# Which engine makes the low parts of the weight slabs in the first block's projections, and how densely the index work is packed

## The reference, cut to what matters

```
u = rmsnorm(h, attn_norm[l])
aq, ak, av, iq, ik, iw, bq, bk, bv, cq, ck, cv, gates = split_columns(u @ w_in)
qa, ka, iqr = rope(aq), rope(ak), rope(iq)
ikr = rope(rmsnorm(ik))
# for each block of 128 queries:
rel   = relu(iqr . ikr * 64**-0.5)              # 8 index heads
score = sum over heads of iw * rel, causal
idx   = top_k(score, 128)                       # the 128 keys that branch A may see
```

## Time and profile before

| what | us |
|---|---|
| median of three runs (lowest, highest) | 3960.11 (3956.6, 3968.04) |
| the profiled execution's own time | 3949.7 |
| its span | 3947.9 |
| busy in the span: PE, DVE, ACT, POOL | 3495.5, 1724.7, 1390.2, 926.9 |
| GpSimd's low parts of these slabs (L448), 32 of them | 148.9 |
| VectorE's low parts of these slabs (L448), 4 of them | 2.29 each |

### The profile page before, as it was taken

One profiled execution on the slowest core, in us unless ns is written; L12 is line 12 of the kernel. 1 busy time (PEld: TensorE's weight loads), 2 busy tenths in 40 slices (PEclk: granted clock), 3 DMA queues, 4 the chain that ended last, 5 costly groups with the idle time before them and its releaser, 6 DMA issues. The chain is left out here.

```text
span 3947.9 us, 53824 instructions
## 1 busy us (share of the span) xinstructions
PE 3495.5 (89%) x22008; PEld 2731.5 (69%) x22008; DVE 1724.7 (44%) x2477; ACT 1390.2 (35%) x2022; POOL 926.9 (23%) x477
## 2 busy tenths in 40 slices
PE   6978998999798789899979979679997988869997
PEld 4755786888576568688857549558884836748885
DVE  6686334322369643441323544444413544443433
ACT  5536332322354443232324342244313343224422
POOL 3327001444342620044433220011102321011100
PEclk9989999999999899999989979889998978979999
DMA  3200221222121022222222000212222100012221
GB/s 126 86 22 24 82 99 71 102 86 96 74 86 43 1 81 101 76 87 96 96 92 86 22 1 4 75 54 96 96 75 81 65 0 2 24 64 85 96 96 53
DMA packets 38648, 266.57 MB, mean 68 GB/s; under 512 B 4784, under 2 KB 5040, under 8 KB 7472
## 3 DMA queue, kind: packets, MB, share of 16 engines
q1 hardware_dynamic: 38448, 263.74, 18.8%
HBM read 261.63 MB, written 2.10 MB: 67 GB/s over the span
## 5 line engine op out<-in xcount | busy, mean ns | idle before, releaser
L1150 POOL TENSOR_TENSOR w_lo_f<-raw_f,w_hi_f 128x2048 fp32r<-128x2048 f32 x64 | 296.0, 4624 | 910.7 <-ACT w_hi_f L360 910.7
L372 PE MATMUL ps<-u_hi,w_hi_d 128*128 128x512 f32 x832 | 327.7, 394 | 93.1 <-DVE w_lo_d L366 54.0
L373 PE MATMUL ps<-u_lo,w_hi_d 128*128 128x512 f32 x832 | 326.6, 392 | 0.0
L374 PE MATMUL ps<-u_hi,w_lo_d 128*128 128x512 f32 x832 | 326.3, 392 | 0.0
L366 DVE TENSOR_TENSOR w_lo_d<-raw_d,w_hi_d 128x2048 fp32r<-128x2048 f32 x74 | 169.5, 2292 | 283.6 <-ACT w_hi_d L360 283.6
L372 PEld LDWEIGHTS ps<-u_hi,w_hi_d 128*128 128x128 f32 x832 | 158.1, 190 | 129.5 <-DVE w_lo_d L366 55.6
L372 PE MATMUL ps<-u_hi,w_hi_f 128*128 128x512 f32 x512 | 202.9, 396 | 33.2 <-DVE u_lo L350 33.1
L360 ACT ACTIVATE w_hi_d<-raw_d 128x2048 fp32r<-128x2048 f32 x74 | 140.9, 1907 | 247.0 <-PE ps L374 241.1
L360 ACT ACTIVATE w_hi_f<-raw_f 128x2048 fp32r<-128x2048 f32 x64 | 122.5, 1914 | 264.3 <-PE ps L374 249.6
L851 POOL TENSOR_SCALAR sc<-sc,small 128x768 f32<-128x768 f32 (+4 forms) x144 | 174.2, 1225 | 155.3 <-DVE small L916 155.3
L374 PE MATMUL ps<-u_hi,w_lo_f 128*128 128x512 f32 x512 | 203.8, 398 | 0.0
(11 more groups left out here) (375 smaller groups left out, 8175.8 us busy)
## 6 DMA issues: line engine op xcount, KB each, us to landing
raw_d<-in_w SPq DMA_DIRECT2D x74, 1024.0 KB, 4.8
raw_f<-in_w SPq DMA_DIRECT2D x64, 1024.0 KB, 4.8
raw_c<-in_w SPq DMA_DIRECT2D x40, 1088.0 KB, 5.0
raw_a<-in_w SPq DMA_DIRECT2D x36, 1024.0 KB, 4.8
raw_p<-in_w SPq DMA_DIRECT2D x24, 1024.0 KB, 4.9
cst<-in_cst SPq DMA_DIRECT2D x1, 2112.0 KB, 8.0
h<-in_x SPq DMA_DIRECT2D x8, 256.0 KB, 4.4
mla_w<-in_w SPq DMA_DIRECT2D x2, 1024.0 KB, 6.8
```

The source lines that it names most:

```text
L372: nc.tensor.matmul(out, w_hi, x_hi, start=start, stop=False)
L373: nc.tensor.matmul(out, w_hi, x_lo, start=False, stop=False)
L374: return nc.tensor.matmul(out, w_lo, x_hi, start=False, stop=stop)
L1150: nc.gpsimd.tensor_tensor(WF[2][:, k % 2, :], WF[0][:, k % 2, :], WF[1][:, k % 2, :].bitcast(F32), ALU.subtract).then_inc(S["w_lo"], 1)
```

## The change

`INDEX_AT` becomes 8 + i // 2, so two pairs of index heads follow each of the tiles n = 8 to 13, on all three engines. VectorE makes up to three picks after a tile. All low parts are made by VectorE: those of slabs 0 and 1 at the start, that of slab 2 after the rope of tile 1, and those of later slabs each in the place that `split_a_hi` has in ScalarE's order: after the ropes, index work and picks of slab i comes the low part of slab i + 3. GpSimd makes only the low parts of the activations.

```diff
-            INDEX_AT = [8 + i for i in range(len(INDEX))]
+            INDEX_AT = [8 + i // 2 for i in range(len(INDEX))]
+            def index_after(n):
+                return [INDEX[i] for i, at in enumerate(INDEX_AT) if at == n]
...
             def slab_ready(pe, i):
-                if i < 2:
-                    pe.wait_ge(S["w_lo"], i + 1)
-                else:
-                    pe.wait_ge(S["slab_lo"], i - 1)
+                pe.wait_ge(S["w_lo"], i + 1)
...
-            def split_a_lo(eng, i, done):
-                eng.wait_ge(S["w_hi"], i + 1)
-                eng.tensor_tensor(WA_lo[:, i % 4, :], WA_raw[:, i % 4, :], WA_hi[:, i % 3, :].bitcast(F32), ALU.subtract)\
-                   .then_inc(done, 1)
+            def split_a_lo(dve, i):
+                if i < len(SLABS):
+                    dve.wait_ge(S["w_hi"], i + 1)
+                    nc.vector.tensor_tensor(WA_lo[:, i % 4, :], WA_raw[:, i % 4, :], WA_hi[:, i % 3, :].bitcast(F32),
+                                            ALU.subtract).then_inc(S["w_lo"], 1)
...
                 @block.gpsimd
                 def _(pool):
                     split_u_lo(pool, four)
-                    for i in range(2, len(SLABS)):
-                        split_a_lo(nc.gpsimd, i, S["slab_lo"])
...
                     rope_bank(0, 1)
+                    split_a_lo(dve, 2)
...
-                    for n, t in enumerate(TILES):
-                        if n < 2:
-                            continue
-                        rope_bank(n, t)
-                        if n - 1 in INDEX_AT:
-                            index(*INDEX[INDEX_AT.index(n - 1)])
-                        for _ in range(2):
-
-                            if row is not None and n - 1 >= INDEX_AT[row * IDX_HEADS // 2 - 1]:
-                                row = next(picks, None)
+                    for i, k in enumerate(SLABS):
+                        if i in VPAIR:
+                            split_a_lo(dve, i + 3)
+                            split_a_lo(dve, i + 4)
+                        elif i - 1 not in VPAIR:
+                            for t in (2 * k, 2 * k + 1):
+                                if not 1 < t < N_QK:
+                                    continue
+                                n = TILES.index(t)
+                                rope_bank(n, t)
+                                for at in index_after(n - 1):
+                                    index(*at)
+                                for _ in range(3):
+
+                                    if row is not None and n - 1 >= INDEX_AT[row * IDX_HEADS // 2 - 1]:
+                                        row = next(picks, None)
+                            split_a_lo(dve, i + 3)
```

More of the change, by code:

```diff
@@ L420, in build @@
                         n = TILES.index(t)
-                        if n in INDEX_AT:
-                            b, hp = INDEX[INDEX_AT.index(n)]
+                        for b, hp in index_after(n):
                             for e in range(2):
@@ L509, in _ @@
                                 n = TILES.index(t)
-                                if n in INDEX_AT:
-                                    index(*INDEX[INDEX_AT.index(n)])
+                                for b, hp in index_after(n):
+                                    index(b, hp)
                 @block.scalar
@@ L587, in _ @@
                     own = Signal(dve_own)
-                    split_a_lo(nc.vector, 0, S["w_lo"])
-                    split_a_lo(nc.vector, 1, S["w_lo"])
+                    split_a_lo(dve, 0)
+                    split_a_lo(dve, 1)
                     dve.wait_ge(loaded, 16)
```

## The result

The changed kernel takes 3972.72 us (median of 8 runs, 3965.41 to 3983.85); the kernel before, over 8 runs, 3961.74. The ratio is 1.0033, 95% interval 1.0017 to 1.0048: **slower by 0.33%**, a little and clearly. The forecast was 3961, no change; the measured time lies outside its near range of 3951 to 3969 us and at the very end of the wide one of 3945 to 3973. The kernel was run again twice for the experiments: ratios 1.0018 (1.0004 to 1.0031) and 1.0036 (1.0023 to 1.0049).

What follows compares the result with a forecast made beforehand. TensorE, busy 89% of the span, was taken as the bound, VectorE close behind. Layers +1.7 and +0.2, attention -2, clock +1.5 sum to +1.4, giving 3961 us; range 3951 to 3969, 8 in 10 from 3945 to 3973.

Steps and rivals of the forecast that it cites:

- The relief of VectorE: VectorE's steps with two SBUF inputs stop being held up: some 2 us or more per low part.
- V0 without a stall: Before V0 in layer 1, TensorE's 2.4 us stall goes, with 0.8 us to spare; V0 ends at 111.2.
- Rival C: Slab 5's low part comes late, V0 starts up to 2.4 us late as now: 3965; chance 0.07.
- The banks: Five banks per tile of n = 8 to 13 make five TensorE bubbles, some 9 us per layer.
- VectorE's sum: VectorE's work from tile 10's swap to slab 17's low part: 117.2 us, leaving a 19 us stall before V1.
- The third pick: Three picks per tile from n = 10: last of 48 made at n = 25, no tail left.
- The clock in the bubbles: Clock falls from the five bubbles cost 0 to 8 us per layer; +1.5 taken for both layers together.
- the 0.9 that the prediction names as a sign of being wrong: The prediction calls itself wrong if the clock in 125 to 170 us falls below 0.9.
- rival B: Index tiles' bubbles make TensorE's clock fall; ten falls cost 8 us per layer, about 3975; chance 0.10.
- VectorE's waits: Between V0 and V1, VectorE idles about 2 us waiting for the swaps of tiles 12 and 14.
- The attention's start: Without 15 us of idle TensorE before it, the attention gains 1 us per layer by the clock: -2.
- The median: The runs' median lies 10.4 above the profiled execution of 3949.7; that difference is carried over to the forecast.

Runs made afterwards that it cites:

- e3: The changed kernel with two picks per tile instead of three; 3947.42 us, ratio 0.9972 to the kernel before.
- e7: The changed kernel with slab i + 3's low part ahead of the picks of slab i's last tile; 3966.75 us, ratio 1.0011 to the kernel before.
- e5: The kernel before with VectorE making all low parts, one pair of heads and two picks per tile; 3936.46 us, ratio 0.9933.
- e10: The changed kernel with two picks per tile, and two pairs of heads only after tiles 8 and 9; 3926.61 us, ratio 0.9934 to the kernel before.
- e6: The kernel before with three picks per tile and nothing else of the change; 3954.49 us, ratio 0.9982.
- e8: The changed kernel with heads read before the swap and added before the rope, two picks per tile; 3936.77 us, ratio 0.9927 to the kernel before.

## Why the prediction was wrong, point by point

*The relief of VectorE.* Right. The rope's middle step (now L601) is held up nowhere, by the groups of VectorE from 111.5 to 262 us, where its mean was 1.61:

```profile
L601 DVE TENSOR_TENSOR four<-four,sin 128x512 f32<-128x512 f32 x17 | 11.6, 681 | 0.0
```

*V0 without a stall.* Right: TensorE goes on without a break, and V0's last values come at 111.6 us (111.2 forecast). Rival C did not occur.

*The banks.* Right in kind and place: five bubbles of 1.1 to 1.9 us, forecast 1.5 to 2. Together they are 7.2 us and not 9.

*VectorE's sum.* Right. From 135.6 to 261.9 us it does what I counted as 117.2 us in 117.7 (126.3 less 8.6 of idleness). Counted the same way, from the rope of tile 10 to V1 less the waits, the four other profiles with this order give 117.6 to 117.8. In e3, with 15 picks fewer, it is 95.3 (22.2 us of picks less by the sum), in e7, with three fewer, 113.0 (4.6 less by the sum). So a pick taken out shortens the chain by its own length, and V1 follows until TensorE is met, as in e3 and e5. The stall before V1 is 19.1 us, as forecast, but it tests less than the whole sum: TensorE already waits 0.5 us for slab 15's low part at 231.53, so the stall is the time from there to slab 17's part less two tiles, whatever came before.

*The third pick.* Followed from the sum and well forecast, but only as a fact of the change. The rows would also have said that it is harmful: V1 is the cover for 15 picks, which the change emptied.

*The clock in the bubbles.* This is the step that failed: "From 0 to 8 us per layer; I take +1.5 for both together, near the rows of 1.21 us without one." Measured in its place: 5.1 us lost in each layer, 10.2 together; 10.2 and 6.8 together in the two other profiles of this kernel. From 125 to 170 us the mean clock was 0.89, below the 0.9 that the prediction names as a sign of being wrong. The mechanism was named, as rival B, with a fitting price for one short fall (1.6 us; measured 1.7, and 3.4 for a fall of double length), but it was given a chance of 0.10 and said to decide only from about seven falls on; there were four, two of them of double length. I rated a bubble by its own length, beside four single stalls, and these were too few to rate it by: the first bubble of a layer, 1.87 us long, had a fall right behind it in 9 of 14 passes over the profiles of the kernels that have it. In e10, where it is the only one, that was so in both layers, so it doesn't take five in a row. The Trainium skill's page "TensorE: Matmul & The Clock Gate", section "A second HAM failure mode: psum-queue depth-cycling", on small idle times from cycling through PSUM banks, was nearer to the truth than my weighing of it: all six stretches with the bubbles show falls, those with filled bubbles none.

*VectorE's waits.* "It idles about 2 us" was short as well: it was 8.6. The filled runs split this: 3.9 us are there without any fall, 4.7 come with the falls. So of the 7.6 us by which V1 came late (261.9 and not 254.3), 4.7 are the clock, 1.9 are waits that I counted too low, 0.5 is the later start of the chain (135.6 for 135.1) and 0.5 the work itself (117.7 for 117.2).

*The attention's start.* Also wrong: "I take 1 us per layer: -2". TensorE now comes from V1 with only the barrier's 1.8 us of idleness, and in layer 1 the first 4.3 us of the attention have a mean clock of 0.63 where it was 0.50, with TensorE busy for 3.6 of them and not 4.3. But nothing of that arrives later: from the attention's start to the first merge slab it takes 129.8 us, 129.4 before. In layer 2 the last merge slab comes 342.9, 339.6 and 342.9 us after it in the three profiles of this kernel, 337.8 before, and 337.8 to 344.0 in all the profiles in which TensorE stood idle for 7 us or more before the attention. A gain of 1 us could not be seen in that spread; the profiles show none.

*The median.* The step from the profiled execution to the median was loose: the profiled execution of before (3949.7) lies 12 us below the median of its 8 runs, that of the change (3975.1) 2 above. The two stages' +16.3 us between the two profiles is an upper figure for medians 11 apart. Part of that spread is in the unchanged second block, which lasted from 1885.9 to 1907.3 us over all these profiles.

So the sum was right in what it counted, and short in what it estimated: +1.4 forecast, +11.0 measured. What the profiles show is where V1 and the attention start; how much of the 11.0 is the clock's, no pair of medians here says.

## What to carry to other kernels

Before giving a helper's work to an engine with a queue in fixed order, list what then stands ahead of it in that queue: the same three picks per tile were a small gain with GpSimd making the low parts (e6) and a stall of 19 us in VectorE's queue. Where the other engine has a long stretch of work ahead, leave as much deferrable work for it as it covers: V1 covers about 15 picks, and the kernels that leave them to it (e5, e8, e10) are the fastest here. Count PSUM banks when work is packed more densely, and price repeated short idle times of TensorE with the clock and not by their length.

## What was not expected of the hardware

Bubbles of 1.1 to 1.9 us, 9 to 13 us apart, brought the granted clock from 1.00 to 0.50 between one and four times per layer, behind other bubbles from one execution to the next, for 3.4 or 6.8 us each, while TensorE was busy for about 90% of the stretch. A single bubble of 1.87 us did it too, in both layers of e10. The same stretch with the bubbles filled had no fall. And the kernel with a few more TensorE instructions in the first block took 3 to 4 us longer per layer in one stretch of the second, in both its profiles, for reasons that no run here shows.
